# Hybrid trunk on one core: where token transposes, the first state hop and half a table level stand in the RWKV rounds

## The reference, cut to what matters

```python
def _rwkv7(r, k, v, w_lr, a_lr, w0, w2, a0, a2, k_k, k_a, r_k, ln_g, ln_b):
    ...
    kk = kk / jnp.maximum(jnp.linalg.norm(kk, axis=-1, keepdims=True), 1e-12)
    k = k * (1.0 + (a - 1.0) * k_a.reshape(hs))

    def step(state, inp):
        rt, wt, kt, vt, kkt, at = inp
        sa = jnp.einsum('bhvk,bhk->bhv', state, -kkt)
        state = state * wt[:, :, None, :] + sa[..., None] * (kkt * at)[:, :, None, :] + vt[..., None] * kt[:, :, None, :]
        return state, jnp.einsum('bhvk,bhk->bhv', state, rt)
    ...
    _, y = lax.scan(step, s0, (tm(r), tm(decay), tm(k), tm(v), tm(kk), tm(a)))

def _even_layer(...):
    z = (h @ w_in).astype(jnp.float32)
    ...
    oa = _rmsnorm(_hgrn2(qa, fa, ia, lb), ...)
    ob = _rwkv7(rb, kb, vb, wlr, alr, w0, w2, a0, a2, k_k, k_a, r_k, ln_g, ln_b)
    y = jnp.concatenate([oa, ob], axis=-1) * jax.nn.silu(gate)
    return y.astype(x.dtype) @ w_out
```

## Time and profile before

| | |
|---|---|
| three runs | 1206.3, 1210.14, 1210.93 us; median 1210.14 |
| the profiled execution | 1209.45 us; its span, first to last instruction, 1207.4 us |
| busy share of the span | PE 95%, PE weight loads 75%, DVE 63%, POOL 52%, ACT 37% |
| chain that ended last | PE 77%, DVE 15%, ACT 3%, issue 3% |
| mean granted clock of TensorE | 0.993 |

### The profile page before, as it was taken

How to read it: one execution, slowest core, us unless ns; L and a number is a source line. 1 busy time by engine, 2 the same in 40 slices (tenths; PEclk the granted TensorE clock), 3 DMA queues, 4 the chain that set the end, 5 groups by cost and what they waited for, 6 DMA issues and landing times.

```text
span 1207.4 us, 31001 instructions
## 1 busy us (share of the span) xinstructions
PE 1150.2 (95%) x12066; PEld 908.5 (75%) x12066; DVE 756.6 (63%) x1334; ACT 441.9 (37%) x834; POOL 626.7 (52%) x594
## 2 busy tenths in 40 slices
PE   1899999999999999999999999998999999999996
PEld 0677778777778787777787778876677777777874
DVE  6656565675675656846765441638468686876537
ACT  4333342343333423433335420225235344352224
POOL 3644343452443534524435567866557475748863
PEclk9999999999999999999999999999899999999998
DMA  6221121121211211212212143322222231313321
GB/s 212 70 73 54 46 64 56 54 70 32 64 56 46 65 53 55 71 31 63 63 46 65 53 140 113 96 90 87 76 71 87 70 87 61 92 57 96 96 87 69
DMA packets 46889, 88.70 MB, mean 73 GB/s; under 512 B 5824, under 2 KB 7104, under 8 KB 46528
## 3 DMA queue, kind: packets, MB, share of 16 engines
q1 hardware_dynamic: 44496, 82.37, 22.7%
q10 hardware_dynamic: 2288, 4.72, 1.2%
HBM read 84.97 MB, written 2.10 MB: 72 GB/s over the span
## 4 chain that ended last, share of the span: by engine, by line
PE 77%; DVE 15%; ACT 3%; issue 3%; DMA 1%; SPq 0%; DVEq 0%; ACTq 0%
PE psum L377 74%; DVE mix L1645 3%; ACT mix L1117 3%; DVE mix L1669 1%; DVE mix L2257 1%; DVE h_split L1649 1%; DVE mix L2235 1%; PE psum L1021 1%; DVE mix L2244 1%; DVE mix L2255 1%; PE psum L516 1%; DMA mix<-xT 1%; ACT L1117 0%; DVE mix L2343 0%; DVE psum L1734 0%
## 5 line engine op out<-in xcount | busy, mean ns | idle before, releaser
L377 PE MATMUL psum<-h_split,w_hi 128*128 128x512 f32 x2320 | 751.0, 405 | 15.6 <-DVE h_split L1649 11.0
L377 PEld LDWEIGHTS psum<-h_split,w_hi 128*128 128x128 f32 x2320 | 423.1, 189 | 122.8 <-issue 25.4
L331 POOL TENSOR_SCALAR w_hi<-w_raw 128x512 fp32r<-128x512 f32 x290 | 208.9, 720 | 520.4 <-PE psum L377 370.1
L377 PE MATMUL psum<-h_split,w_lo 128*128 128x512 f32 x1160 | 456.3, 393 | 0.0
L333 POOL TENSOR_TENSOR w_lo<-w_raw,w_hi 128x512 fp32r<-128x512 f32 x290 | 405.7, 1399 | 24.2
L1117 ACT ACTIVATE mix<-psum 128x512 f32<-128x512 f32 (+4 forms) x292 | 140.6, 495 | 396.8 <-PE psum L377 251.4
L377 PEld LDWEIGHTS psum<-mix 64*64 64x64 f32 (+3 forms) x8256 | 230.3, 138 | 73.7 <-issue 51.7
L377 PE MATMUL psum<-mix 64*64 64x64 f32 (+5 forms) x8256 | 272.0, 236 | 7.2 <-ACT mix L1117 2.3
L377 PEld LDWEIGHTS psum<-h_split,w_lo 128*128 128x128 f32 x1160 | 219.1, 189 | 48.0
L1117 ACT ACTIVATE mix<-mix 128x512 f32<-128x512 f32 (+2 forms) x253 | 128.8, 541 | 123.6 <-DVE mix L2127 48.0
L1734 DVE COPY_PREDICATED mix<-mask,psum 128x128 f32<-128x128 uint8 (+1 forms) x192 | 83.0, 470 | 41.6 <-PE psum L377 39.3
(11 more groups left out here) (132 smaller groups left out, 666.6 us busy)
## 6 DMA issues: line engine op xcount, KB each, us to landing
w_raw<-wall SPq DMA_DIRECT2D x290, 256.0 KB, 2.6
mix<-xT SPq DMA_DIRECT2D x4, 512.0 KB, 5.3
mix<-xT ACTq DMA_DIRECT2D x1, 2048.0 KB, 8.1
out<-mix SPq DMA_DIRECT2D x7, 256.0 KB, 2.6
mix<-mask_f SPq DMA_DIRECT2D x1, 1728.0 KB, 10.6
mix<-pT ACTq DMA_DIRECT2D x2, 512.0 KB, 3.7
mix<-lru_w ACTq DMA_DIRECT2D x4, 256.0 KB, 3.1
mix<-w2a ACTq DMA_DIRECT2D x16, 32.0 KB, 2.2
```

Source lines behind the costliest of these rows:

```text
L331: pool.tensor_scalar(w_hi[:, slot, :, :], w_raw[:, slot, :], 1.0, 0.0, ALU.mult, ALU.add).then_inc(sem["w_hi"], 1)
L377: return pe.matmul(o, lhsT, rhs, start=start, stop=stop, skip_group_check=True)
```

## The change

Three edits. On PE, in rounds 1 to 7, the four transposes of levels 2 and 3 move from behind N to between P and N. The first hop writes bank 5 in place of bank 7, so that it no longer waits for `state_readers`; the wait is put on the second hop, which writes bank 7. On DVE, in rounds 1 to 7, part 1 of table level 3 moves from in front of `hop_state(4)` to behind `hop_add(5)`. In `last_round` only the hop's bank and wait change.

```diff
+        def hop_bank(c):
+
+            return (H1 if c == 1 else R1)[:, 0:64]
...
                 if c == 1:
                     pe.wait_ge(sem["rw_np"], count("rw_np", r))
                     pe.wait_ge(sem["rw_mt"], count("rw_mt", r))
-                    pe.wait_ge(sem["rw_rp"], count("rw_rp", r))
                 else:
                     pe.wait_ge(sem["rw_s"], count("rw_s", r, c - 2))
-                mm(R1[:, 0:64], m_t[:, c, :], state(c)).then_inc(sem["rw_c"], 1)
+                    if c == 2:
+                        pe.wait_ge(sem["rw_rp"], count("rw_rp", r))
+                mm(hop_bank(c), m_t[:, c, :], state(c)).then_inc(sem["rw_c"], 1)
...
                         if lvl == 4:
                             value_rows(r)
+                        else:
+                            token_rows(r, lvl, True)
                         inverse_n(r, lvl, 0)
                         inverse_n(r, lvl, 1)
-                        if lvl < 4:
-                            token_rows(r, lvl, True)
                         t(3, 2 * lvl - 2, 2 * lvl)
...
-                stt(s_all[:, c + 1, :], R1[:, 0:64], e_pos[:, c, RL:RL + 1], s_next, ALU.mult, ALU.add).then_inc(sem["rw_s"], 1)
+                stt(s_all[:, c + 1, :], hop_bank(c), e_pos[:, c, RL:RL + 1], s_next, ALU.mult, ALU.add).then_inc(sem["rw_s"], 1)
...
                     hop_add(r, 4)
-                    between(level, 3, (1,))
                     hop_state(r, 4)
                     hop_add(r, 5)
+                    between(level, 3, (1,))
                     hop_state(r, 5)
```

## The result

The changed kernel took 1201.01 us (median of 6 runs, 1198.42 to 1203.06). The kernel before, run again beside it, took 1206.75 us (median of 6, 1205.81 to 1210.93). The medians are 5.74 us, or 0.48%, apart. The ratio, which goes by the means (1207.73 and 1200.90), is 0.9944, with a 95% interval of 0.9929 to 0.9959: 0.56% faster, about 6.8 us. The profiled execution took 1203.06 us, its span is 1201.1.

A forecast was written before the change was run, and what follows sets the result against it. PE, busy 95% of the span, was taken as the bound, losing time at a few waits. Transposes 2.4, first hop 3.4, fourth state 2.0, less 0.3, save 7.5 us: 1210.14 to 1202.6 us, range 1200.0 to 1207.0.

The forecast's parts named there:

- The level: Starting time of the sum: the kernel before at its three-run median of 1210.14 us, giving 1202.6 us after the change.
- the border of faster: Time below which the result counts as faster by more than 0.5%: 1204.1 us, 1.5 us above the forecast.
- The cover of hop 6: PE at hop 6: its state allows a start at 382.85, PE wants it at 382.93; cover 0.08 us, nothing deducted.
- The transposes: PE, levels 2 and 3, rounds 1 to 7: block 2.30 us instead of 2.47, 0.17 us a level, 2.4 us total.
- The first hop: PE at hop 1: without the wait for state_readers, 0.48 us a round gained, 3.4 us in 7 rounds.
- The weights of hop 2: PE at hop 2: weights may come late, so 0.05 us a round is taken off, 0.3 us total.
- The fourth state: PE, hop 4 to hop 5: 1.34 us instead of 1.62 with hop_state(4) earlier, 0.28 us a round, 2.0 us total.
- What edit 2 moves: Freeing hop 1 of its wait was to move PE, DVE and POOL all 0.48 us forward among the hops.
- faster by more than 0.5%: Outcome class given 64%, against 34% for same and 2% for slower by more than 0.5%.
- partly lost: Rival, 24%: hops 5, 2 or 6 keep or take over a wait, or transposes bring nothing; 1204.8 us.
- Nothing: Rival, 6%: a chain through ACT and DVE between rounds is the true bound, PE waits elsewhere; 1210.1 us.
- The slower one: Rival, 4%: POOL's w_lo starts just ahead of the moved products, hop 6 loses 1.2 us a round; 1210.9 us.

The follow-up runs named there:

- the split transposes: Changed kernel with the four transposes of levels 2 and 3 in two pairs, one between the halves of P, one behind them: 1204.62 us, one run.
- the version with small work in the gaps: Changed kernel with 64-row work between P and N at levels 2 to 4, transposes back behind N, both key masks on DVE at level 2: 1196.84 us.
- `w_hi` three times more: Changed kernel with POOL's w_hi of every fourth weight unit computed three more times, so w_lo comes 2.5 us later: 1212.82 us, one run.
- `w_hi` once more: Changed kernel with POOL's w_hi of every fourth weight unit computed once more, so w_lo comes 0.8 us later against the hops: 1207.33 us, one run.

## Why the prediction came out as it did: what held, and which steps failed

The forecast was 1202.6 us, with a saving of 7.5; measured were 1201.01 and, by the rounds, 6.9 (6.8 by the means of the times, 5.7 by the medians). The direction and the three mechanisms came out, each shown by itself. Two steps of the sum failed.

**The level.** "... on the median to 1202.6 us": the sum hangs on the median of three runs, 1210.14 us, and so do the lower end of the range and the border of faster. The same kernel came to 1206.75 in six runs and 1207.5 in twenty, so this term was 3.4 us too high.

**The cover of hop 6.** The prediction took nothing off for it, on two grounds. One is "Edit 2 moves both sides 0.48 us forward, and POOL with them"; the other is that a state is early enough when the hop itself can start, 0.33 us after its `hop_state`. The runs show neither as it was said. It gives back 0.04 us a round, 0.3 us in all.

Step by step:

1. **The transposes.** The rows gave 2.30 us for the block, and it takes 2.30. Over a round the edit brings 0.29 to 0.31 us instead of 0.34, so 0.15 a level instead of 0.17, 2.2 us instead of 2.4. The price of a visit to full-size work is shown by the split transposes: 0.48 - 0.17 = 0.31 us a level in the prediction's terms, 0.31 measured. Without that price the edit would have brought three times as much; the version with small work in the gaps, which adds no such visit, has most of that.
2. **The first hop.** 0.48 us forecast at hop 1, 0.48 measured. Neither `rw_np` nor `rw_mt` took over. (`rw_np` comes from `state_sums`, which is two instructions ahead of L1911 and not one, so it was there still earlier.) That the wait alone costs is shown with the hop in bank 5 and the wait kept.
3. **The weights of hop 2.** 0.05 us a round taken off, about 0.02 measured.
4. **The fourth state.** 0.28 us forecast; from hop 4 to hop 5 it takes 1.34 us instead of 1.62, as forecast, and 0.26 a round for the edit alone. `hop_add(4)` stayed slow, as the earlier trace rows had it.
5. **Hop 6.** `hop_state(5)` starts at 380.34, its result lets the hop go at about 380.67 and PE reached it at 380.73, so the hop's start is not held, but the slices behind it start 0.18 us after it, not 0.14: the second of the hop's two passes is late. Single passes in the timelines show what it goes by. It starts 0.49 us after the start of its `hop_state`, wherever that is later than 0.06 after the first: 0.39 + 0.10 here, 0.36 + 0.12 with `w_hi` three times more, 0.42 + 0.07 at hop 2, 0.33 + 0.16 at hop 6 with `w_hi` once more. From about 0.44 on, the two passes are 0.06 apart in every kernel. (Hop 5, which stands behind table passes of another shape, has 0.16 in any case.) So a hop wants its state 0.44 us ahead and not 0.33, and a cover of 0.08 was 0.03 short even as it was worked out.
6. **What edit 2 moves.** Against `state_sums`, hop 4 moves 0.46 us forward (5.29 to 4.83) and `w_lo` only 0.41 (4.83 to 4.42). The kernels with the first hop's edit alone and with both hop edits have the new distances; those with the transposes alone, with the fourth state alone and with the wait kept in bank 5 have the old ones. The link is on POOL: `w_hi` starts over a table product of DVE (379.16 to 379.58 before, 376.97 to 377.39 now), takes 0.71 and 0.75 us instead of 0.62, and ends 0.48 and 0.47 us behind that product, and `w_lo` follows it. DVE has no idle time left between `state_sums` and that product, so it can't move by the whole 0.48. That puts `hop_add(4)`, the moved products and `hop_state(5)` 0.05 us later against PE. With the fourth state early but the wait on hop 1, alone or in bank 5, hop 6 gives back only 0.00 to 0.02 us.

Together, in a round: 0.31 + 0.48 + 0.28 less 0.06 for hops 2 and 6 is 1.01 us, and the round itself says 0.99, 6.9 us in 7. The prediction had 1.07 a round; its own terms, 0.34 + 0.48 + 0.28 - 0.05, are 1.05 or 7.35 us, which the rounding of each made 7.5.

A saving of 7.5 on 1206.75 would have been 1199.3, below my lower end of 1200.0 (1202.6 less half the spread of the three runs, 2.3, is 1200.3). That the measured time lies in the range, 1.6 us under the forecast, is luck: it is the sum of errors of opposite sign, a level 3.4 too high and a saving 0.7 too large, and of 1.1 us by which the median of the changed kernel lies above what its rounds say. Nor did "faster by more than 0.5%", to which the prediction gave 64%, come out clearly: the medians are 0.48% apart, and the interval of the ratio, 0.41 to 0.71%, lies on both sides of that border.

Why the level is loose is shown in part. PE's stops in blocks of 64x64 passes differ from execution to execution: behind level 5 of the last round alone the traces have between 2.94 and 4.59 us for the same 128 passes. The granted clock drops to the lower of its levels for short stretches as well, and how many of them a run has, and where, differs: three in the profiled execution of either kernel, beside one near the end that all have, and a single one in that of the transposes alone, which with 1202.63 us took less than the changed kernel's 1203.06. The clock isn't the whole of it: three runs of the changed kernel with the same mean clock of 0.993 took 1200.04, 1202.74 and 1203.06 us. Two stretches of 10 to 50 us, first of the kernel before, then of the changed one (busy times and counts, then the granted clock, share of the DMA, GB/s):

```profile
10.00:50.00 40.00, 23.17 (x82) 16.04 (x83) 27.41 (x29) 16.96 (x25) 21.58 (x20) 1.00 0.38 132
```

```profile
10.00:50.00 40.00, 23.22 (x77) 16.21 (x78) 27.23 (x28) 16.21 (x24) 20.63 (x19) 0.96 0.37 129
```

One of its three stretches lies ahead of the first round in the changed kernel, and none in the kernel before. Its first `state_sums` is 1.0 us later, at 135.85 instead of 134.88; a stop of PE at level 4 just ahead of it, 2.41 us instead of 2.09, is 0.3 of that, and whether the clock is the rest isn't shown. From the last one to the end it takes 511.85 instead of 513.35. So the two spans differ by 6.3 us, of which the rounds hold 5.8.

Of the rivals, "partly lost" names the true kind of deviation: thin covers at hops 2 and 6. But no wait came back, and what they lose, 0.4 us, is far from the 2.0 and more that it priced. "Nothing" is excluded by the interval. The slower one has its mechanism, DVE's instructions ending behind POOL's, at work in every kernel here. In the changed kernel `w_lo` starts 0.41 us ahead of hop 4, where it was 0.46, so it meets `hop_add(4)` as before; where I shifted POOL it cost 0.17 and 0.41 us a round.

## What to carry to other kernels

When PE is busy throughout, compare starts of neighbouring matmuls in places with and without a wait: it finds losses that the table of waits understates or doesn't show, and it sizes them to some hundredths. To fill a gap between small matmuls, look first for work of their own shape; work of another shape pays for two changes of shape. When a cover is worked out, find out from the rows how early the data must be for the matmul behind not to be late either, and check that every engine moves by the whole gain. And hang the forecast of a small gain on more than three runs, or widen its lower end by what their median may be off.

## What the runs showed that I had not expected

- It isn't only `w_lo` (two inputs) on POOL that holds up DVE's instructions with both inputs in SBUF. `w_hi`, which has one input, goes with slower ones too: `hop_add(4)` took 0.54 us instead of 0.28 and ended 0.06 behind it, and the product of 128x256 took 0.83 instead of 0.42 beside it. It goes the other way as well: `w_hi` takes 0.71 to 0.75 us instead of 0.62 where it starts over such a product.
- A late state costs in two ways: it can hold the hop itself, and a hop that starts on time can still push the slices behind it, by 0.01 to 0.06 us in the kernels with the first hop's edit, because its second pass starts 0.49 us after the start of the `hop_state` at the earliest.
- Single rounds are 0.1 to 0.9 us longer than the value that repeats, in every kernel, without a change in the order of the work. In the places named above PE stops within a block of 64x64 passes, for 0.2 to 1.5 us, and waits for nothing that the profile names. The cause stays open.
